# Moving half of a token compression among the projections that it shares TensorE with, and swapping three accumulators

## The reference

```python
(cq, ckv, kr, fq, fk, fv, ff, nq, nkc, nvc, nks, nvs, nkw, nvw, ng) = jnp.split(h @ w_in, split_points, axis=-1)

def nsa_compress(tok, pos_emb, w1, w2):          # for keys, then for values
    blk = tok[:, idx] + pos_emb[None, None, :, None, :]      # 15 blocks of 32 tokens
    blk = blk.transpose(0, 1, 3, 2, 4).reshape(B, n_cmp, G, NSA_CMP_LEN * D)
    return jax.nn.gelu(blk @ w1) @ w2                        # w1 is 4096 x 512

k_cmp = nsa_compress(kc, pos_k, ck_w1, ck_w2)
v_cmp = nsa_compress(vc, pos_v, cv_w1, cv_w2)
o = jnp.concatenate([rms_norm(o_mla, g_mla), rms_norm(o_fox, g_fox), rms_norm(o_nsa, g_nsa)], axis=-1)
x = x + gt_a * (o @ w_out)
```

## Time and profile before

| | |
|---|---|
| median of 3 runs | 2435.87 us (2433.2 to 2439.37) |
| profiled execution | 2436.38 us |
| its span, first to last instruction | 2434.5 us |
| around the span | 1.9 us |
| mean granted clock of TensorE | 0.989 of full speed |
| PE, DVE, ACT busy | 96%, 71%, 47% of the span |

### The profile page before, as it was taken

One profiled execution on the slowest core, in us unless ns is written; L12 is line 12 of the kernel. 1 busy time (PEld: TensorE's weight loads), 2 busy tenths in 40 slices (PEclk: granted clock), 3 DMA queues, 4 the chain that ended last, 5 costly groups with the idle time before them and its releaser, 6 DMA issues.

```text
span 2434.5 us, 29301 instructions
## 1 busy us (share of the span) xinstructions
PE 2327.7 (96%) x11145; PEld 1912.0 (79%) x11145; DVE 1718.7 (71%) x2094; ACT 1139.3 (47%) x1584; POOL 19.2 (1%) x52
## 2 busy tenths in 40 slices
PE   3798999999999999999999999999999999999998
PEld 2686778778888888888878777888788888888887
DVE  7985788889787787887767667786666555555455
ACT  3253355545534434434446445454553453443453
POOL 1000000000000000000000000000000000000000
PEclk9799999999999999999999999999999999999999
DMA  9979986889889899898878798466677666666653
GB/s 367 384 257 337 332 283 204 270 295 329 286 303 313 298 329 321 299 327 300 299 239 273 252 319 279 152 217 208 211 258 239 183 188 196 185 189 191 190 186 126
DMA packets 318611, 633.90 MB, mean 260 GB/s; under 512 B 20428, under 2 KB 41352, under 8 KB 317832
## 3 DMA queue, kind: packets, MB, share of 16 engines
q1 hardware_dynamic: 314432, 625.49, 76.8%
q10 hardware_dynamic: 4040, 6.54, 0.8%
HBM read 629.85 MB, written 2.10 MB: 260 GB/s over the span
## 4 chain that ended last, share of the span: by engine, by line
PE 82%; DVE 7%; DMA 5%; ACT 2%; issue 2%; SPq 1%; POOL 0%; ACTq 0%; POOLq 0%; DVEq 0%
PE acc L1740 18%; PE acc L1742 17%; PE acc L1741 17%; PE pair L1740 7%; PE pair L1742 7%; PE pair L1741 7%; DVE ada_acc L1183 3%; DMA w_raw<-in_w_in 2%; DMA arena<-in_ada_w 2%; DVE w_lo L1256 2%; PE bank_T L1600 1%; PE acc L1764 1%; PE pair L1791 1%; PE bank_O L1600 1%; ACT w_hi L774 1%
## 5 line engine op out<-in xcount | busy, mean ns | idle before, releaser
L1256 DVE TENSOR_TENSOR w_lo<-w_raw,w_hi 128x1024 fp32r<-128x1024 f32 (+3 forms) x764 | 906.4, 1190 | 399.0 <-ACT w_hi L774 397.6
L774 ACT ACTIVATE w_hi<-w_raw 128x1024 fp32r<-128x1024 f32 (+3 forms) x764 | 785.4, 1031 | 755.2 <-PE acc L1742 437.1
L1740 PE MATMUL acc<-w_hi,hT_hi 128*128 128x512 f32 (+3 forms) x1536 | 611.6, 398 | 28.9 <-DVE w_lo L1256 12.4
L1742 PE MATMUL acc<-w_lo,hT_hi 128*128 128x512 f32 (+3 forms) x1536 | 590.6, 385 | 0.0
L1741 PE MATMUL acc<-w_hi,hT_lo 128*128 128x512 f32 (+3 forms) x1536 | 590.0, 384 | 0.0
L1183 DVE SCALAR_TENSOR_TENSOR ada_acc<-w_raw,silu_c,ada_acc 128x1024 f32<-128x1024 f32 x300 | 383.5, 1278 | 1.1 <-DVE small L1336 0.4
L1740 PEld LDWEIGHTS acc<-w_hi,hT_hi 128*128 128x128 f32 x1536 | 292.1, 190 | 101.2 <-DVE w_lo L1256 21.9
L1742 PEld LDWEIGHTS acc<-w_lo,hT_hi 128*128 128x128 f32 x1536 | 291.9, 190 | 56.3
L1741 PEld LDWEIGHTS acc<-w_hi,hT_lo 128*128 128x128 f32 x1536 | 292.7, 191 | 51.2 <-issue 1.7
L1740 PE MATMUL acc<-w_hi,uT_hi 128*128 128x512 f32 (+1 forms) x656 | 257.0, 392 | 0.0
L1742 PE MATMUL acc<-w_lo,uT_hi 128*128 128x512 f32 (+1 forms) x656 | 254.7, 388 | 0.0
(11 more groups left out here) (256 smaller groups left out, 1927.2 us busy)
## 6 DMA issues: line engine op xcount, KB each, us to landing
w_raw<-in_mlp_w SPq DMA_DIRECT2D x512, 512.0 KB, 4.8
w_raw<-in_ada_w SPq DMA_DIRECT2D x320, 512.0 KB, 5.7
w_raw<-in_w_in SPq DMA_DIRECT2D x112, 512.0 KB, 5.3
arena<-in_ada_w SPq DMA_DIRECT2D x64, 512.0 KB, 11.2
w_raw<-in_w_out SPq DMA_DIRECT2D x64, 512.0 KB, 5.6
w_raw<-in_nsa_cmp_k_w SPq DMA_DIRECT2D x32, 512.0 KB, 6.7
w_raw<-in_nsa_cmp_v_w SPq DMA_DIRECT2D x32, 512.0 KB, 6.4
w_raw<-in_w_in SPq DMA_DIRECT2D x16, 388.0 KB, 5.3
```

What stands on the lines that cost most here:

```text
L774: a.activation(w_hi[:, at % RING, :, 0:n], w_raw[:, i % RAW, :, 0:n], ACT.Copy).then_inc(hi_done, 1)
L1256: v.tensor_tensor(w_lo[:, at % RING, :, 0:n], w_raw[:, RING_NO["lo", Q] % RAW, :, 0:n], w_hi[:, at % RING, :, 0:n].bitcast(F32), ALU.subtr ...
L1740: pe.matmul(o, st_hi[:, kt + k, tok], wh, start=first and k == 0, stop=False)
L1742: mm = pe.matmul(o, st_hi[:, kt + k, tok], wl, start=False, stop=last and k == 1)
```

## The change

The second half of `cw1` (pieces 17 to 32) is given other places: its pairs now stand behind one, three, two and two pieces of `nqa`, behind three, two and three pieces of `nqb`, and behind the first piece of `fq`. `fq` and `fv` go from `acc[1]` to `acc[0]`, `fk` from `acc[0]` to `acc[1]`. `wo0` and `wo1` change places in the order. The read-out of `nqb` is listed for place 99, not 104; `hpre` 1 and `hid1` for 103, not 101 and 102.

```diff
-    "fq": ("w_in", 832, 512, 1), "fk": ("w_in", 1344, 512, 0), "fv": ("w_in", 1856, 512, 1),
+    "fq": ("w_in", 832, 512, 0), "fk": ("w_in", 1344, 512, 1), "fv": ("w_in", 1856, 512, 0),
...
-ORDER += ["vw", "cw1"] * 7 + ["vw", "cw1", "cw1"] + ["nqa", "cw1"] * 7 + ["nqa", "cw1", "cw1"]
-ORDER += ["nqb", "cw1"] * 5 + ["nqb"] * 3
-ORDER += ["fq"] * 8 + ["fk"] * 8 + ["fv"] * 8
-ORDER += ["wo0"] * 2 + ["wo1"] * 2 + ["wo0"] * 4 + ["wo1"] * 4 + ["wo2"] * 6 + ["wo0"] * 2 + ["wo1"] * 2
+ORDER += ["vw", "cw1"] * 7 + ["vw"]
+for name, count in (("nqa", 1), ("nqa", 3), ("nqa", 2), ("nqa", 2), ("nqb", 3), ("nqb", 2), ("nqb", 3), ("fq", 1)):
+    ORDER += [name] * count + ["cw1"] * 2
+ORDER += ["fq"] * 7 + ["fk"] * 8 + ["fv"] * 8
+ORDER += ["wo1"] * 2 + ["wo0"] * 2 + ["wo1"] * 4 + ["wo0"] * 4 + ["wo2"] * 6 + ["wo0"] * 2 + ["wo1"] * 2
...
-                    (56, "kv1"), (72, "vw"), (89, "nqa"), (104, "nqb"), (112, "fq"), (120, "fk"), (128, "fv")):
+                    (56, "kv1"), (72, "vw"), (89, "nqa"), (99, "nqb"), (112, "fq"), (120, "fk"), (128, "fv")):
...
-    side(F + 101, ("hpre", l, 1), 1)
+    side(F + 103, ("hpre", l, 1), 1)
...
-             (81, "kcmp"), (91, "nqa0"), (92, "nqa1"), (96, "cum"), (102, "hid1"), (105, "nqb0"), (106, "nqb1"),
+             (81, "kcmp"), (91, "nqa0"), (92, "nqa1"), (96, "cum"), (103, "hid1"), (105, "nqb0"), (106, "nqb1"),
```

## The result

The changed kernel takes 2466.19 us (median of 4 runs, 2462.37 to 2469.91), against 2436.65 us for the kernel before in the same comparison. The ratio is 1.0121, interval 1.0107 to 1.0135: slower by 29.5 us. The prediction said 2457, with a range of 2443 to 2470. In the file after, every line number from L774 on is one higher (L1740 is L1741, L1791 is L1792, L927 is L928).

A forecast was written before the change was run, and what follows sets the result against it. PE, busy 96% of the span, was taken as the bound, with only idle time, clock and order able to move. 3.5 + 3.8 + 10.7 - 1.9 + 5.1 = 21.2 us on 2435.9 gave 2457, range 2443 to 2470.

The forecast's parts named there:

- (a): From `vw` to `nqa` on `acc[0]`: the read-out comes late, stalls of 2.1 and 1.4 us, 3.5 us in sum.
- (b): From `nqa` to `nqb`: read-out behind slot 7, `rms` and two `lo`; 5.2 us idle per layer, 3.8 us added together.
- (c): From `nqb` to `fq`, slots 9 to 12: waits of 3.5, 1.7, 1.1 and 0.4 us per layer; 10.7 us added.
- (d): Late `w_lo` of `nqa` in layer 0, 2.2 us before: 1.9 us won back.
- (e): Clock: layer 0 keeps three low times, layer 1's gaps bring three more at 1.7 us: 5.1 us, bounds 0 and 10.
- (f): Accumulator swap, `wo0` and `wo1`, `hpre`, `hid1`: zero cost, covered by at least six pieces of over 2.7 us.
- Faster: DMA paces both layers; with sparser pairs, pieces land in time: -8 to -12 us, 2426; chance 0.04.
- the range's upper rival: Every gap over 2.5 us brings two low times and slots 12, 13 slip: +28 to +35 us, 2468; chance 0.18.

The follow-up runs named there:

- the kernel with the exponential first: The changed kernel with slot 8's exponential ahead of the read-out of `nqb` within place 99: 2462.22 us.
- the second half alone: The kernel before with only the change's `nqb` and `fq` part, swapped accumulators, read-out of `nqb` at 100: 2453.87 us, ratio 1.0082.
- the first half: The kernel before with only the change's `vw` and `nqa` order, the four pairs left among `nqb`: 2444.26 us, ratio 1.0037.
- all the moves but `hid1`: The changed kernel with read-outs of `vw` at 70, `nqa` at 84, `kcmp` ahead of the latter, slots 9 to 13 later: 2452.76 us.
- the first half with its hand-overs mended: The kernel of the first half with `vw` read out at 70, `nqa` at 84 and `kcmp` ahead of it: 2434.42 us, ratio 0.9994.

## Why the prediction was right, point by point

The sign and most of the size were right: 21.2 us forecast, 29.5 measured. The measured 2466 us lies in the range, but not in the 2449 to 2465 that belonged to the forecast itself. The two stretches grew by 27.5 us in the profile, to 125.4 and 126.7 us where 123 and 121 were forecast. The terms, with both layers taken together:

| step | forecast, us | profile after, us |
|---|---|---|
| (a) `vw` to `nqa` | 3.5 | 2.6 + 1.9 = 4.5 |
| (b) `nqa` to `nqb`, added | 3.8 | 6.5 + 6.3 - 3.5 - 3.1 = 6.2 |
| (c) slots 9 to 12 | 10.7 | 4.6 + 4.1 - 2.7 = 6.0 |
| (d) late `w_lo` | -1.9 | 0.4 - 2.2 = -1.8 |
| (e) clock | 5.1 | 9.9 |
| (f) swap, `hpre`, `hid1` | 0 | 2.7 |

The terms miss by +1.0, +2.4, -4.7, +0.1, +4.8 and +2.7 us, 6.3 in sum. That the total came this near is in part luck: (c) was put too high by about what (e) was put too low, and only some of that is one cause, the half speed behind slot 9's gap told under (c).

**(a)** held in place and nearly in size. Moving the read-out to 70 left 0.9 us, the bare copies that were its lower bound.

**(b)** named the right chain and was 1.2 us short per layer. In layer 1 that is the modulation tile (1.2 us) between `lo(87)` and `lo(88)`; the step took the two `lo` at 1.14 us between starts from a place with no tile. In layer 0 no tile stands there, but `lo(86)` waited 1.1 us for its weights and pushed slot 7 back. The reading of the 3.5 and 3.1 us of before was incomplete too: with the read-out moved in the kernel before, 2.8 us stay, in layer 0 for weights that land late, in layer 1 for them and for the rest of the read-out step on DVE. The trace names only what came last.

**(c)** was right on slot 9: 3.5 forecast, 3.4 measured. For slots 10 and 11 it gave 1.7 and 1.1 us, where the trace has 0 and 0.7. Their chain is hardly faster: slot 10's exponential is done 7.4 us behind the last `nqb` product in layer 1, where 7.9 were forecast. PE is slower: it arrives at slot 10 after 8.9 us, not 6.2. Beside the 3.4 us gap the clock is at 0.50 for 6.8 us, in layer 0 from 1.3 us before its end, and this holds slot 9, the pair and the value products:

```profile
323.06:329.89 6.83, 5.57 (x22) 3.29 (x23) 4.51 (x9) 3.55 (x11) 0.00 (x0) 0.50 0.21 60
```

What the step charged as idle time PE spent at half speed, and it went into step (e). Slot 12 has no wait where 0.4 was forecast; 0.6 of layer 0's 4.6 us belongs to slot 13, which the step did not name. One small slip of the prediction stands under its rival *Faster*: the three bare operations of (c), 1.02, 1.28 and 0.9, make 6.4 us over both layers, not 6.6. That the wait belongs to the chain and not to the read-out is shown by the kernel with the exponential first.

**(d)** held within 0.1 us. One of its two reasons is borne out: in the five kernels whose read-out of `vw` stands at 70, so that the stall of (a) is 0.9 us, a late `w_lo` of 1.1 us is back in layer 0.

**(e)** was mis-sized. Outside idle time the stretches lost 27.5 - 17.6 = 9.9 us, not 5.1. The trace has eleven low times (3.41 us each at a clock of 0.50) in them where before it had four: three more were forecast, seven came. Seven at 1.7 us would be 11.9; taking off the parts that lie over idle time leaves 8.2, and the other 1.7 us is not assigned. The gaps of 6.5 and 6.3 us and both 3.4 us gaps of slot 9 have two low times each beside them, those of 2.6, 1.9 and 2.7 us one each. The prediction left layer 0 its three, where five are, and gave layer 1 three more, where five more are; it counted none for the gaps of (a). The Trainium skill ("TensorE: Matmul & The Clock Gate", section "Why this matters for your kernels") warns of idle gaps between bursts of matmuls, and these two stretches agree with it at the four gaps of 3.4 us and more. They show low times beside three shorter gaps too, at which the page's warning does not yet aim; and other kernels here have gaps of 2.2 and 2.4 us with none.

**(f)** had one wrong zero. The swap itself costs nothing: no wait for `fk`, `fv`, `wo0` or `wo1` appears. But `hid1`, moved from 102 to 103 and behind the last pair, shares `bank_T` with `adaG1a`, and the step asked only about accumulators. Its 2.7 us also bring a low time. The place is shown by the kernel with `hid1` earlier, where the wait falls to 0.4 us; the second half alone has it as well.

Nor was the range's upper rival (all gaps charged twice, slots 12 and 13 late, 2468) far off: four of the six gaps over 2.5 us had two low times, and the measured time lies between it and the forecast. That the waits are local and not one limit of the stretch is shown in part. The totals of the two halves add up, and the first half costs nothing more once its two hand-overs are mended. The second half was not mended: each move there traded a wait for another, and whether some order of its slots would be free of them stays open.

## What to carry to other kernels

When a chunk is moved, ask at each shared buffer, PSUM transpose banks included, what now stands between its last writer and its reader in every engine's program; a step moved to mend one engine takes its part on the others with it. A wait in a profile names the last of several late things, so before taking it away look when the next one (here the weights' landing, and in one layer the rest of the moved step itself) would have let the engine go. A gap on TensorE can also cost clock: here 17.6 us more idle time came with 9.9 us more of busy time for the same work, 8.2 of them by the clock's rows.

## What was not expected of the hardware

One gap of layer 0 lies outside the change, before the first scores behind 440 us (L1784 in the kernel before, L1785 in the changed one; its place is in the second row). It is followed by a granted clock of 1.00 in the kernel before, in that with the read-out of `nqa` at 87, and in the one with the exponential first. In the changed kernel and the ten others the clock beside it is 0.50 for 3.4 or 6.8 us. The three that go free are 3.38, 3.28 and 3.21 us long, the eleven others 3.37 to 3.42. The kernel before (free) and the one with the read-out of `nqa` at 84 (6.8 us at 0.50):

```profile
442.05 0.49 PE L1784 MATMUL pair<-arena 128*128 128x128 f32 x2 [3.38 <-ACT arena L927]
```

```profile
449.73 0.79 PE L1785 MATMUL pair<-arena 128*128 128x128 f32 x2 [3.37 <-ACT arena L928]
```

Two of the three free ones are the shortest of all, but these two rows are the same length to 0.01 us, so the length of the gap does not decide it. Gaps of 1.9 to 2.7 us in the changed stretches have a low time beside them, while one of 2.4 us does not (slot 9 in layer 1 of the kernel with all the moves but `hid1`), and neither does one of 2.2 us (slot 8 in layer 0 of the first half with its hand-overs mended). One and the same gap thus cost between nothing and 3.4 us of clock, and the clock's share of a change could be told only in bounds. What decides it no run here shows.
